# Every eighth row product of a PEER gather moved from VectorE to GpSimd and ScalarE

## The chip, the cores and the metric

The kernel runs on one core of a Trainium2 chip. The metric is device time in microseconds (us) for one execution, the median of several runs.

## The reference, cut to what matters

One decoder layer is computed for 1024 prompt tokens and 8 sample tokens: a retention and a sliding-window attention group, an output projection, and then the PEER block, whose inner part is what the change touches. For each token, eight heads pick 16 of 16384 experts each, so 128 experts per token, and

```python
h = jnp.einsum('thkd,td->thk', peer_u[idx], xt)
a = jax.nn.gelu(h, approximate=False) * gates
return jnp.einsum('thk,thkd->td', a, peer_v[idx])
```

with d = 1024 in float32. Each token thus needs 128 rows of `peer_u` and 128 rows of `peer_v`. The kernel has the two tables side by side, one row of 8 KB per expert.

## The kernel before, in words

The prompt's tokens are worked in 8 blocks (`NB`) of 128, one token per partition. In each block there are 128 *units* (`SLOTS`): a unit is one expert for each of the 128 tokens. Its row pair (u beside v, 128 partitions x 8 KB, 1 MB in all) is fetched by one indirect DMA that GpSimd issues (`fetch`, line 657) into one of 8 places of a ring (`RING`; place r = unit % 8). Tokens are split between even and odd units so that each fetch brings rows for two half sets; hence the two operand tiles `xlo` and `xhi`, for even and odd units.

A unit then goes through four engines:

- VectorE, `expert_dot` (line 1943): waits for the row's landing (`ld_row[r]`), multiplies the u half by the token (`xlo` or `xhi`) and adds up along the row in the same instruction, into `dot[:, r]`. After each odd unit it raises `dots`, one count per pair of units.
- ScalarE, `weigh` (line 1402), once per pair p: waits for `dots`, takes the gelu of both sums, and writes two 128x64 diagonals over the u half of the row. It raises `diags`.
- TensorE, `add_pair` (line 1093, matmuls at line 1097), once per pair: waits for `diags` and adds diagonal times v half into the block's sum in PSUM, eight matmuls by the profile's count. Each of the two units raises `used` with its last matmul.
- GpSimd: for unit u it waits for `used` to say that unit u - 8 is done with the place, and issues the next fetch.

GpSimd's program (line 676 on) is one plain loop over blocks, quarters and units. At the start of each quarter of 32 units it also waits for the picked indices to be moved (`moved`) and copies them (`take_picks`, line 669, with a wait for its own copy). It does nothing else until the 8 fetches for the sample tokens at the end.

All other work of the layer (projections of later tiles, the attention of the next block, the picking of its experts, the output norm) is interleaved by hand in ticks: after each unit or pair an engine calls `advance`, which runs the steps that fall due at that tick. So TensorE's program order is pair, other work, pair, other work, and the same holds on VectorE and ScalarE; nothing is reordered at run time. Plain loads and stores are issued from the SP queue, by the same ticks.

At the start of a block, `take_over` on VectorE (line 1930) and `take_halves` on ScalarE (line 1417) wait for all dots of the block before, since they overwrite `xlo` and `xhi`.

Of the kernel before, what the change touches and what calls it, by code (L numbers as in the profile page):

```python
# [9 lines left out]
ALU = mybir.AluOpType  # L10
# [3 lines left out]
P = 128  # L14
# [127 lines left out]
def build(nc, A, out):  # L142
    ctx = ExitStack()
    with ctx:
# [3 lines left out]
        def sem(name):  # L148
            return ctx.enter_context(nc.semaphore(name))
# [174 lines left out]
        ld_first, ld_const, ld_skT = sem("ld_first"), sem("ld_const"), sem("ld_skT")  # L324
        ld_g1, ld_xT_first, ld_xT_early = sem("ld_g1"), sem("ld_xT_first"), sem("ld_xT_early")
        ld_wq = [sem(f"ld_wq{i}") for i in range(QG)]
# [31 lines left out]
        halves_taken = sem("halves_taken")  # L358
        head_moved = sem('head_moved')
        moved = [sem(f"moved{i}") for i in range(QTR)]  # L360
        ld_row = [sem(f"ld_row{r}") for r in range(RING)]
# [25 lines left out]
        def _(sp):  # L387
# [161 lines left out]
            sp.dma_start(xT_first, A["xT"][0]).then_inc(ld_xT_first, 16)  # L549
            sp.dma_start(g1c, A["norm1_g"].rearrange("(k p) -> p k", p=P), allow_slow_non_contiguous=True).then_inc(ld_g1, 16)  # L550
            load_w(0)
# [102 lines left out]
        def _(pool):  # L654
# [6 lines left out]
            picks_in = stage[:].bitcast(U32)  # L661

            def take_first_head():

                hold(pool, head_moved, 32)
                nc.gpsimd.tensor_copy(idxg[:, 0, :, 0:HPAIRS], picks_in[:, 0, :, 0, 0:HPAIRS]).then_inc(idx_taken, 1)
                hold(pool, idx_taken, 1)
# [10 lines left out]
            for b in range(NB):  # L678
                for quarter in range(QTR):
                    if b == quarter == 0:  # L680
                        take_first_head()
                    else:
                        take_picks(b, quarter, 0)
                    for unit in range(quarter * QSLOTS, (quarter + 1) * QSLOTS):
                        if b == 0 and unit == 2 * HPAIRS:
                            take_picks(0, 0, HPAIRS)
                        if b == 0 and unit == RING // 2:
                            hold(pool, pj_mm, NCH + AHEAD)
                        hold(pool, used, b * SLOTS + (unit + 1))
                        pick = unit // 2 % QPAIRS  # L690
                        fetch(unit % RING, idxg[:, quarter, unit % 2, pick:pick + 1])

            pool.wait_ge(sm["idx8"], 1)
# [460 lines left out]
        def _(act):  # L1154
# [247 lines left out]
            def weigh(b, p):  # L1402
                r = 2 * p % RING
                act.wait_ge(dots, b * PAIRS + (p + 1))
                me.did(nc.scalar.activation(gel[:, r:r + 2], dot[:, r:r + 2], ACT.Gelu))  # L1405
                me.sync()
# [10 lines left out]
            def take_halves(b):  # L1417

                if b:
                    act.wait_ge(dots, b * PAIRS)  # L1420
                    act.nop(nofuse=True)
                act.wait_ge(x2_swapped, b + 1)
# [66 lines left out]
        def _(v):  # L1489
# [78 lines left out]

            v.wait_ge(ld_g1, 16)
            v.nop(nofuse=True)  # L1570
            v.wait_ge(ld_xT_first, 16)
            gain(xT_first)
# [357 lines left out]
            def take_over(b):  # L1930

                if b:
                    v.wait_ge(dots, b * PAIRS)
                    v.nop(nofuse=True)
                v.wait_ge(x2_swapped, b + 1)
                me.did(nc.vector.tensor_copy(xlo[0:HP, :], x2[0:HP, :]))
# [6 lines left out]
            def expert_dot(b, unit):  # L1943
# [3 lines left out]
                          accum_out=dot[:, r:r + 1])  # L1947
                if unit % 2:
                    ins.then_inc(dots, 1)
# [31 lines left out]
            for b in range(NB):  # L1981
                take_over(b)
                for unit in range(SLOTS):
                    expert_dot(b, unit)
                    if b and unit == 3:
# [156 lines left out]
```

## Time and profile before

| what | value |
|---|---|
| median of 3 runs | 2977.24 us (2976.3 to 2979.08) |
| the profiled execution's own time | 2974.54 us |
| its span | 2972.7 us |
| PE, DVE, ACT, POOL busy | 2245.8, 2075.9, 1094.1, 1207.3 us |
| DMA | 1214.41 MB, mean 409 GB/s |
| mean granted TensorE clock | 0.871 of full speed |

PE is TensorE (PEld its weight loads), DVE VectorE, ACT ScalarE, POOL GpSimd, SP the queue of plain DMAs. A time is that of one profiled execution, counted from its span's start. "Idle before" a row, and what follows the arrow, is the time the engine stood still before that instruction and what ended it. The 1024 units of the ring run from about 131 us to 2946 us, which is 2815 us, 2.75 us a unit; before it lies the first tile's front, behind it the sample tokens' end.

### The profile page before, as it was taken

Reading aid. Unit: us, or ns where it says so; the run is one execution under the profiler, and the core shown is the slowest. Engines: PE = TensorE matmul, PEld = TensorE weight load, DVE = VectorE, ACT = ScalarE, POOL = GpSimd, SP = SyncE. Lnnn points to the kernel's source line nnn. Section 1 sums busy time; section 2 is a strip of 40 time slices with the busy share of each in tenths; the row PEclk is TensorE's granted clock in tenths of the full one; section 3 lists DMA queues with packets and bytes.
Section 4 is the critical chain, followed back from the end, with each engine's and each line's share of the span. In section 5 each row is a group of like instructions: output and inputs, shape, how many; then the busy total and the mean of one; then the engine's idle time right before and its main releaser. Section 6 shows DMA issues by size and latency. Waiting matters only on the chain.

```text
span 2972.7 us, 33489 instructions
## 1 busy us (share of the span) xinstructions
PE 2245.8 (76%) x10572; PEld 1116.2 (38%) x10572; DVE 2075.9 (70%) x5291; ACT 1094.1 (37%) x3330; POOL 1207.3 (41%) x1069
## 2 busy tenths in 40 slices
PE   8898888566899678996776676866786568778755
PEld 6666534122466224662343232512242123314211
DVE  3685458964786557865578865797569865986975
ACT  2233433352343433433434352343434353332322
POOL 0133344444433343334444444444444444544453
PEclk9999889889999788997898788977898789977776
DMA  9999999999999999999999999999999999999998
GB/s 366 381 418 408 399 421 420 408 421 420 416 397 396 424 420 414 400 386 410 421 421 396 421 405 419 421 409 421 415 421 418 411 412 417 420 405 381 412 415 353
DMA packets 197043, 1214.41 MB, mean 409 GB/s; under 512 B 28320, under 2 KB 47592, under 8 KB 63104
## 3 DMA queue, kind: packets, MB, share of 16 engines
q0 software_dynamic: 148608, 1082.20, 88.4%
q1 hardware_dynamic: 48256, 130.07, 11.2%
q8 instruction: 83, 1.36, 0.2%
q14 instruction: 96, 0.79, 0.1%
HBM read 1192.48 MB, written 20.23 MB: 408 GB/s over the span
## 4 chain that ended last, share of the span: by engine, by line
DMA 36%; DVE 28%; PE 23%; issue 5%; ACT 5%; POOL 2%; DVEq 0%; SPq 0%; POOLq 0%; ACTq 0%
DMA ring<-in_peer_uv,idxg 29%; DVE ring L1946 15%; PE ps L1097 11%; PE ps L751 5%; DVE columns L1779 3%; DMA proj_scratch<-wo 3%; POOL ring L657 2%; DVE columns L1773 2%; PE ps L1050 2%; ACT ring L1158 2%; DMA wo<-in_xT_sample 1%; DVE columns L1785 1%; PE ps L1000 1%; DVE columns L1849 1%; PE ps L724 1%
## 5 line engine op out<-in xcount | busy, mean ns | idle before, releaser
L657 POOL DMA_INDIRECT ring<-in_peer_uv,idxg x1024 | 1185.4, 1158 | 1613.1 <-PE ps L1097 1417.3
L1097 PE MATMUL ps<-ring 128*64 128x512 f32 x4096 | 1227.3, 729 | 659.3 <-ACT ring L1158 647.2
L1946 DVE SCALAR_TENSOR_TENSOR ring<-ring,xlo 128x1024 f32<-128x1024 f32 x512 | 627.5, 1226 | 367.6 <-DMA ring<-in_peer_uv,idxg 323.2
L1946 DVE SCALAR_TENSOR_TENSOR ring<-ring,xhi 128x1024 f32<-128x1024 f32 x512 | 627.4, 1225 | 322.7 <-DMA ring<-in_peer_uv,idxg 300.6
L1097 PEld LDWEIGHTS ps<-ring 128*64 128x64 f32 x4096 | 285.1, 156 | 1357.8 <-ACT ring L1158 928.1
L1405 ACT ACTIVATE small<-small 128x2 f32<-128x2 f32 x512 | 103.8, 203 | 1494.2 <-DVE ring L1946 1479.8
L1050 PEld LDWEIGHTS ps<-work,wq 128*128 128x128 f32 x2304 | 274.0, 196 | 87.8 <-issue 86.5
L1158 ACT ACTIVATE ring<-gdiag,small 128x64 f32<-128x64 f32 x1024 | 300.3, 340 | 16.8
L1158 ACT ACTIVATE gdiag<-fold,gateg 128x64 f32<-128x64 f32 x1024 | 293.0, 333 | 3.0
L1050 PE MATMUL ps<-work,wq 128*128 128x128 f32 (+1 forms) x2304 | 292.9, 281 | 1.1 <-ACT work L1158 1.1
L751 PE MATMUL ps<-wo 128*128 128x176 f32 x1680 | 272.9, 320 | 13.7 <-ACT wo L1158 6.0
L751 PEld LDWEIGHTS ps<-wo 128*128 128x128 f32 x1680 | 255.1, 193 | 60.1 <-issue 45.3
L1773 DVE MAX8 columns<-columns 128x8 f32<-128x128 f32 (+3 forms) x432 | 116.8, 324 | 41.7 <-ACT columns L1158 37.4
L1779 DVE FIND_INDEX8 columns<-columns 128x8 uint32<-128x128 f32 (+3 forms) x432 | 135.3, 328 | 0.0
L1000 PE MATMUL ps<-wo,work 128*128 128x512 f32 x224 | 109.4, 621 | 0.0
L1405 ACT ACT_TABLE_LOAD x82 | 105.2, 1283 | 1.5
L1158 ACT ACTIVATE wo<-ps,small 128x176 f32<-128x176 f32 (+1 forms) x96 | 40.1, 422 | 148.9 <-PE ps L751 94.7
L1158 ACT ACTIVATE columns<-ps 128x512 f32<-128x512 f32 (+2 forms) x98 | 54.0, 560 | 60.0 <-PE ps L1050 40.4
L1000 PEld LDWEIGHTS ps<-wo,work 128*128 128x128 f32 x224 | 40.0, 193 | 72.4 <-issue 72.4
L1785 DVE MATCH_REPLACE8 columns<-columns 128x128 f32<-128x128 f32 (+3 forms) x216 | 66.9, 319 | 0.0
L1849 DVE TENSOR_TENSOR columns<-columns 128x256 f32<-128x256 f32 (+1 forms) x144 | 54.9, 420 | 2.6
L1852 DVE TENSOR_REDUCE columns<-columns 128x32 f32<-128x512 f32 (+2 forms) x74 | 49.6, 670 | 2.5
(214 smaller groups left out, 1580.9 us busy)
## 6 DMA issues: line engine op xcount, KB each, us to landing
wo<-in_w_in SPq DMA_DIRECT2D x41, 704.0 KB
ring<-in_peer_uv,idxg POOLq DMA_INDIRECT x1024
wo<-in_w_out SPq DMA_DIRECT2D x4, 4096.0 KB, 17.1
ring<-in_w_in SPq DMA_DIRECT2D x8, 1408.0 KB, 7.4
wq<-in_w_q SPq DMA_DIRECT2D x4, 2048.0 KB, 25.2
proj_scratch<-wo SPq DMA_DIRECT2D x93, 88.0 KB
columns<-proj_scratch SPq DMA_DIRECT2D x7, 896.0 KB
h<-in_x_prompt SPq DMA_DIRECT2D x9, 512.0 KB, 7.9
```

What stands on the lines that cost most here:

```text
L657: nc.gpsimd.indirect_dma_start(row[r], None, A["peer_uv"], bass.IndirectOffsetOnAxis(ap=experts, axis=0)).then_inc(ld_row[r], 16)
L751: mm = nc.tensor.matmul(o, tokens_T(n, k), w[:, k, :], start=(k == 0), stop=(k == KC - 1))
L1000: mm = nc.tensor.matmul(F[2 + n][0:rows, :], lhsT, weights[:, k, n * 512:(n + 1) * 512], start=(k == 0), stop=(k == KC - 1))
L1050: mm = nc.tensor.matmul(bank_of(b, n, c)[:, c * P:c * P + rows], wq[:, n, k, c * P:(c + 1) * P], xT[:, k * P:k * P + rows], start=(k == 0) ...
L1097: mm = nc.tensor.matmul(acc[side * HP:(side + 1) * HP, n * 512:(n + 1) * 512], row_u[r][:, 0:HP], row_v[r][:, n * 512:(n + 1) * 512], star ...
L1158: return nc.scalar.activation(o, i, ACT.Copy, **kw_)
L1405: me.did(nc.scalar.activation(gel[:, r:r + 2], dot[:, r:r + 2], ACT.Gelu))
L1773: me.did(nc.vector.max(v16(j)[:, r8 * 8:r8 * 8 + 8], rowsof(j)))
L1779: me.did(nc.vector.max_index(i16(j)[:, r8 * 8:r8 * 8 + 8], v16(j)[:, r8 * 8:r8 * 8 + 8], rowsof(j)))
L1785: me.did(nc.vector.match_replace(rowsof(j), v16(j)[:, 0:8], rowsof(j), TAKEN))
L1849: me.did(tt(o3, o3, i4[:, h0 + hh, c, :].rearrange("p (a k) -> p a k", a=1) .to_broadcast([rows, TK, TK]), ALU.mult))
L1946: ins = stt(row_u[r], row_u[r], 1.0, (xlo, xhi)[unit % 2][:], ALU.mult, ALU.mult, accum_out=dot[:, r:r + 1])
```

## The change

Of every eight units the last (place 7) is taken from VectorE. GpSimd multiplies its u half by `xhi`, in place, and ScalarE adds the products up with a copy that has an accumulator, before its gelu. GpSimd does this between its fetches: after the fetch of the unit with place 5 of the next round, six units later, and for a block's last unit right after that unit's own fetch. `take_over` and `take_halves` also wait for the block's GpSimd products. Apart from this, the first load of the norm weights now raises the same semaphore as the load beside it, which frees one semaphore.

```diff
-            sp.dma_start(g1c, ...).then_inc(ld_g1, 16)
+            sp.dma_start(g1c, ...).then_inc(ld_xT_first, 16)
...
+            def expert_dot(b, unit):
+
+                r = unit % RING
+                hold(pool, halves_taken, b + 1)
+                hold(pool, x2_taken, b + 1)
+                hold(pool, ld_row[r], b * (ROUNDS * 16) + (unit // RING * 16 + 16))
+                nc.gpsimd.tensor_tensor(row_u[r], row_u[r], xhi[:], ALU.mult).then_inc(pool_dots, 1)
...
                         fetch(unit % RING, idxg[:, quarter, unit % 2, pick:pick + 1])
+                        if unit >= RING and unit % RING == RING - 3:
+                            expert_dot(b, unit + 2 - RING)
+                expert_dot(b, SLOTS - 1)
...
             def weigh(b, p):
                 r = 2 * p % RING
                 act.wait_ge(dots, b * PAIRS + (p + 1))
+                if p % (RING // 2) == RING // 2 - 1:
+                    act.nop(nofuse=True)
+                    act.wait_ge(pool_dots, b * ROUNDS + (p // (RING // 2) + 1))
+                    me.did(nc.scalar.activation(row_u[r + 1], row_u[r + 1], ACT.Copy, accum_out=dot[:, r + 1:r + 2]))
+                    me.sync()
...
                 if b:
                     act.wait_ge(dots, b * PAIRS)
+                    act.nop(nofuse=True)
+                    act.wait_ge(pool_dots, b * ROUNDS)
...
-            v.wait_ge(ld_g1, 16)
-            v.nop(nofuse=True)
-            v.wait_ge(ld_xT_first, 16)
+            v.wait_ge(ld_xT_first, 32)
...
                     v.wait_ge(dots, b * PAIRS)
                     v.nop(nofuse=True)
+                    v.wait_ge(pool_dots, b * ROUNDS)
+                    v.nop(nofuse=True)
...
-                if unit % 2:
+                if unit % 2 or unit % RING == RING - 2:
                     ins.then_inc(dots, 1)
...
-                    expert_dot(b, unit)
+                    if unit % RING < RING - 1:
+                        expert_dot(b, unit)
```

## Rows read from the trace of the kernel before

**Rows 1.** The page's DMA line over 40 slices, and its busiest queue.

```profile
DMA  9999999999999999999999999999999999999998
...
q0 software_dynamic: 148608, 1082.20, 88.4%
```

**Rows 2.** The page's chain that ended last, by line.

```profile
DMA ring<-in_peer_uv,idxg 29%; DVE ring L1946 15%; PE ps L1097 11%; PE ps L751 5%; DVE columns L1779 3%; DMA proj_scratch<-wo 3%; POOL ring L657 2%; DVE columns L1773 2%; PE ps L1050 2%; ACT ring L1158 2%; DMA wo<-in_xT_sample 1%; DVE columns L1785 1%; PE ps L1000 1%; DVE columns L1849 1%; PE ps L724 1%
```

**Rows 3.** The page's costliest groups: count, busy us, mean ns, idle before.

```profile
L657 POOL DMA_INDIRECT ring<-in_peer_uv,idxg x1024 | 1185.4, 1158 | 1613.1 <-PE ps L1097 1417.3
L1097 PE MATMUL ps<-ring 128*64 128x512 f32 x4096 | 1227.3, 729 | 659.3 <-ACT ring L1158 647.2
L1946 DVE SCALAR_TENSOR_TENSOR ring<-ring,xlo 128x1024 f32<-128x1024 f32 x512 | 627.5, 1226 | 367.6 <-DMA ring<-in_peer_uv,idxg 323.2
```

**Rows 4.** Windows: length, busy (count) per engine, granted clock, DMA share, GB/s.

```profile
131.00:2946.00 2815.00, 2125.61 (x9953) 1029.97 (x9953) 1996.80 (x5079) 1054.07 (x3246) 1197.80 (x1056) 0.87 1.01 412
345.07:396.12 51.05, 31.85 (x105) 10.72 (x104) 19.96 (x34) 12.33 (x44) 18.38 (x17) 0.77 1.01 424
396.12:436.27 40.15, 31.00 (x121) 12.28 (x120) 23.29 (x39) 14.16 (x45) 20.89 (x19) 0.87 1.01 421
436.27:478.23 41.96, 36.23 (x226) 22.93 (x225) 32.48 (x93) 11.87 (x43) 18.19 (x16) 0.96 1.01 421
478.23:521.31 43.08, 34.99 (x172) 17.01 (x172) 39.51 (x120) 21.37 (x56) 20.26 (x17) 0.90 1.01 419
```

**Rows 5.** The same four windows, instructions of line 1097 alone (PE, PEld).

```profile
345.07:396.12 51.05, 20.61 (x64) 4.73 (x64) 0.77 1.01 424
396.12:436.27 40.15, 18.16 (x64) 4.27 (x64) 0.87 1.01 421
436.27:478.23 41.96, 16.64 (x65) 3.98 (x65) 0.96 1.01 421
478.23:521.31 43.08, 18.70 (x64) 4.44 (x64) 0.90 1.01 419
```

**Rows 6.** Timeline, places 4 to 7 of a round: start, duration, instruction.

```profile
426.81 2.00 PE L1097 MATMUL ps<-ring 128*64 128x512 f32 x8
...
428.50 1.23 DVE L1946 SCALAR_TENSOR_TENSOR ring<-ring,xhi 128x1024 f32<-128x1024 f32 x1 [1.21 <-DMA ring<-in_peer_uv,idxg]
...
429.76 0.20 ACT L1405 ACTIVATE small<-small 128x2 f32<-128x2 f32 x1 [1.82 <-DVE ring L1946]
...
430.64 1.94 PE L1097 MATMUL ps<-ring 128*64 128x512 f32 x8 [1.83 <-ACT ring L1158]
...
430.83 0.94 POOL L657 DMA_INDIRECT ring<-in_peer_uv,idxg  x1 [0.30 <-issue]
```

**Rows 7.** GpSimd's copies of indices: ns min/median/max by line.

```profile
L672 POOL COPY idxg<-stage x32: 203/219/1210, 156.4 to 2850.9; 128x32 uint32<-128x32 uint32 x31, 128x16 uint32<-128x16 uint32 x1
L666 POOL COPY idxg<-stage x1: 196/196/196, 118.7 to 118.7; 128x16 uint32<-128x16 uint32 x1
```

**Rows 8.** Timeline, one such copy and VectorE's instruction beside it.

```profile
1413.63 0.86 POOL L672 COPY idxg<-stage 128x32 uint32<-128x32 uint32 x1
...
1413.22 1.22 DVE L1946 SCALAR_TENSOR_TENSOR ring<-ring,xlo 128x1024 f32<-128x1024 f32 x1
```

**Rows 9.** ScalarE's copy of 1024 columns and its read of an accumulator, by form.

```profile
L1158 ACT ACTIVATE work<-ps 128x1024 f32<-128x1024 f32 x32 | 32.2, 1008 | 9.1 <-PE ps L702 5.6 <-PE ps L1097 3.5
...
L1251 ACT ACTIVATION_READ_ACCUMULATOR h<-h,small 128x1 f32 x32 | 6.0, 187 | 0.0
```

**Rows 10.** Timeline: GpSimd's first copy and fetch; a fetch into an empty queue.

```profile
118.73 0.20 POOL L666 COPY idxg<-stage 128x16 uint32<-128x16 uint32 x1 [118.28 <-DMA stage<-moving]
119.89 1.10 POOL L657 DMA_INDIRECT ring<-in_peer_uv,idxg  x1 [0.97 <-POOL idxg L666]
...
1330.32 1.03 POOL L657 DMA_INDIRECT ring<-in_peer_uv,idxg  x1 [8.07 <-PE ps L1097]
...
1335.87 1.23 DVE L1946 SCALAR_TENSOR_TENSOR ring<-ring,xlo 128x1024 f32<-128x1024 f32 x1 [5.32 <-DMA ring<-in_peer_uv,idxg]
```

More of the change, by code:

```diff
@@ L324, in build @@
         ld_first, ld_const, ld_skT = sem("ld_first"), sem("ld_const"), sem("ld_skT")
-        ld_g1, ld_xT_first, ld_xT_early = sem("ld_g1"), sem("ld_xT_first"), sem("ld_xT_early")
+        ld_xT_first, ld_xT_early = sem("ld_xT_first"), sem("ld_xT_early")
         ld_wq = [sem(f"ld_wq{i}") for i in range(QG)]
@@ L359, in build @@
         head_moved = sem('head_moved')
+        pool_dots = sem('pool_dots')
         moved = [sem(f"moved{i}") for i in range(QTR)]
@@ L549, in _ @@
             sp.dma_start(xT_first, A["xT"][0]).then_inc(ld_xT_first, 16)
-            sp.dma_start(g1c, A["norm1_g"].rearrange("(k p) -> p k", p=P), allow_slow_non_contiguous=True).then_inc(ld_g1, 16)
+            sp.dma_start(g1c, A["norm1_g"].rearrange("(k p) -> p k", p=P), allow_slow_non_contiguous=True).then_inc(ld_xT_first, 16)
             load_w(0)
```

## The prediction

> **What bounds the kernel now.** I read the page's DMA line first. It is at nine tenths or more in all but the last slice, and GpSimd's queue of fetches alone takes 88.4% of the 16 engines' span [rows 1]. The windows say it more sharply: over the 2815 us in which the ring runs, the DMA share is 1.01 [rows 4]. So the DMA engines bound the kernel, and the busy shares of VectorE and TensorE are of work that has to fit beside the rows. The chain that ended last goes through VectorE's dot for 15% [rows 2], which would speak for relieving VectorE, but over the same stretch the DMA engines hardly rest, so most of that chain runs beside transfers that set the pace anyway. Then I read the groups for who waits: GpSimd waits 1417.3 us in total for TensorE to free a place, TensorE 647.2 us for ScalarE's diagonals [rows 3]. This is a loop: fetch, land, dot, gelu and diagonal, matmuls, fetch. The ring's eight places cover its latency now. The question is how much the change adds to the loop and how much is in reserve.
>
> **The round, as the change makes it.** Call the four pairs of a round of eight places A, B, C, D; D holds places 6 and 7. In the row of before, C's matmuls end at 428.81; the fetch that goes to place 5 starts at 430.83 and ends at 431.77, while D's matmuls have begun at 430.64 [rows 6]. D starts 1.13 us before that fetch ends. With the change, D cannot start before that fetch has ended, GpSimd has multiplied, and ScalarE has added up. From C's end to D's start there is now a fixed path B:
> - C's end to the end of the fetch to place 5: 431.77 - 428.81 = 2.96 us [rows 6]; with the wait behind it some 3.0.
> - The product on GpSimd. No row shows a GpSimd tensor_tensor of 128x1024. Bounds: VectorE does it in 1.23 us [rows 3], the lower end. GpSimd copies 16 columns in 196 ns and 32 in 203 to 219 ns [rows 7], so 0.4 to 1.4 ns a column; 1024 columns of two operands would be 0.9 to 2.9 us, with the fixed 0.2 us up to 3.1 us, the upper end. I take 2.4 us, two passes at VectorE's 1.2 ns a column, since VectorE's row has the same shape. The copy beside VectorE's two-operand instruction says why two passes: it took 0.86 us and ended at 1414.49, just as VectorE's ended at 1414.44, where such a copy alone takes 0.2 us [rows 7, 8]. GpSimd's reads wait for VectorE's, so they share a way in. For that wait I add 0.3 us: VectorE's dot fills about half of the time of a unit (1.23 of 2.75 us), and half a dot is 0.6 us.
> - ScalarE's sum: 1.01 us for 1024 columns and 0.19 us for the accumulator, 1.2 us [rows 9].
> - From gelu to D's first matmul: 430.64 - 429.76 = 0.9 us [rows 6]; three hand-overs of 0.1 us between engines (428.50 + 1.23 = 429.73 to 429.76 and the like).
> B = 3.0 + 0.3 + 2.4 + 1.2 + 0.9 + 0.3 = 8.1 us.
>
> The Trainium skill, "GPSIMD Engine Reference", Performance versus the Vector engine, gives 4497 ns for a tensor_tensor of 2048 columns, by my halving an estimate of 2.25 us; nothing in this trace shows it, and with it the sum below would be some 16 us lower (0.9 us in half a block, 1.2 us at the ends).
>
> **What a round then takes.** TensorE's program is fixed: A, other work, B, other work, C, other work, D, other work. Only the other work between C and D can lie inside the 8.1 us. With W TensorE's busy time in a stretch, O what of it is not line 1097, a quarter of O lies there, so a stretch of n rounds needs W - O/4 + 8.1 n. I take half a block, 345 to 521 us, whose 176.2 us is the mean length of a sixteenth of 2815; each window has two rounds (64 matmuls of line 1097) [rows 4, 5]:
> - 51.05 us: 31.85 - 11.24/4 + 16.2 = 45.2, so 5.8 to spare;
> - 40.15 us: 31.00 - 12.84/4 + 16.2 = 44.0, 3.8 too long;
> - 41.96 us: 36.23 - 19.59/4 + 16.2 = 47.5, 5.6 too long;
> - 43.08 us: 34.99 - 16.29/4 + 16.2 = 47.1, 4.0 too long.
> The ring holds one round, so what a window has to spare is not saved for the next: 13.4 us are lost in half a block, 16 x 13.4 = 215 us. If it could be saved, the whole ring would say 2125.6 - 898.3/4 + 128 x 8.1 = 2937.8 against 2815 us, 123 us lost [rows 3, 4]; that is the low side of this term.
>
> **The ends of blocks.** GpSimd's product of unit 127 stands right behind that unit's own fetch, and waits for its landing. Queued behind it are the next block's index copy and all its fetches; today they go out while the last rows still land. So the queue runs empty, 7 times between blocks and once before the sample rows. From the time unit 127 could be multiplied: 0.1 hand-over, 2.4 product, 0.2 copy, 0.96 from the copy's end to the fetch, and from a fetch into an empty queue to its dot 1335.87 - 1330.32 = 5.55 us [rows 10]; 9.2 us, where rows now follow each other at 2.75. Lost: 6.45 us each, 52 us. Those 8 rounds are counted in the term above too, at 1.7 us each: 13 back.
>
> **The rest.** VectorE loses 128 dots, 157 us busy; nothing waits for it that the DMA engines would not make wait, since their share is already 1.01: I give it nothing. In the densest window VectorE is at 39.5 of 43.1 us; even if it stands still for both of GpSimd's products there, it has 39.5 + 2 x (2.4 - 1.23) = 41.8 us, below the 47.1 above. ScalarE gains 154 us on 1054 and stays the least used. The added waits in the takeovers lie in the emptied queue's 9.2 us. The merged semaphore waits for the same two loads: nothing; its cover is that both were waited for already. The added cost of a lower clock (0.77 where TensorE was busy 62% of a window, 0.96 at 86%, rows 4) as TensorE idles more is left to the range.
>
> **Sum.** 215 + 52 - 13 = 254 us on the profiled execution's 2974.5, which stands 2.7 under the median: 3231, rounded to 3230 us.
>
> **Rivals.**
> 1. *Only the ends of blocks cost.* The ring's depth hides the late D. The condition is a B under which the windows above have room: the third breaks first, at (41.96 - 31.33)/2 = 5.3 us. For it: GpSimd's product could be at its low end and its fetch to place 5 shorter, as VectorE no longer holds it there. Against: 3.0 + 1.2 + 0.9 + 0.3 are 5.4 before any product. Time: 2977 + 52 - 7 = 3022.
> 2. *The port.* GpSimd's product waits for VectorE's instructions not now and then but nearly each time a whole one, 1.2 us more: B = 9.3. Then the windows give -3.4, 6.2, 8.0, 6.4: 20.6 x 16 = 330, and 8 x 7.6 = 61 for the ends, less 21: 3347. For it: the copy of rows 8, and VectorE busy 32 of 42 and 40 of 43 us in two windows. Against: in the other two it is busy half the time. The Trainium skill, "SBUF — State Buffer", Who interferes with whom, has that a VectorE instruction with two SBUF inputs and a GpSimd one that reads SBUF exclude each other for the whole instruction; by that rule, this is the case, and the trace's 0.86 us copy agrees.
> 3. *VectorE's relief wins (the other side).* Where the chain goes through line 1946, 15% of the span, one eighth of it leaves: 56 us, 2921 us. It decides where VectorE ends last and the DMA engines have room; it needs a DMA share well under 1 there and a B under 5.3. The share of 1.01 in all four windows speaks against it.
> 4. *The change does little*: GpSimd's products hide and the ends overlap other traffic. 2977. Against: the order in GpSimd's program leaves no way around the last unit's landing.
>
> **Chances.** Forecast 0.70 (3230), rival 1 0.09, rival 2 0.16, rival 3 0.03, rival 4 0.02. The product at its lower end, 1.2 us, gives B = 6.9 and 6.2 x 16 = 100, ends 42, less 6: 3113; at its upper end, 3.1, B = 8.8 and 282 + 57 - 18: 3298. The range takes in both and most of rival 2: 3100 to 3350. A measurement of this kernel tells about 0.2% from no change: faster 0.03, same 0.02, slower 0.95.
>
> **What would show it.** Right: 128 GpSimd multiplies of about 2.4 us; DMA share in the ring near 0.92 with engines all but idle for some 6 us at seven block ends; TensorE's wait for line 1158 and ScalarE's for GpSimd grown; D 8 us behind C. Wrong: multiplies of 1.2 us, or D soon behind C with the DMA share still 1.01 inside blocks (rival 1), or VectorE's two-operand dots stretched beyond 1.23 us and setting the pace (rival 2).

## The result: slower by 429 us

| | before | after |
|---|---|---|
| median of the runs, us | 2976.77 (4 runs, 2970.0 to 2979.08) | 3406.08 (4 runs, 3401.77 to 3410.06) |
| ratio, 95% interval | | 1.1438 [1.1416, 1.146] |
| profiled execution's own time, its span | 2974.5, 2972.7 | 3405.99, 3404.2 |
| mean granted TensorE clock | 0.871 | 0.815 |

The direction and the path that costs the time came out as forecast, the size did not: 254 us were forecast, 429 measured, which is 175 us more and outside the range.

The page of the changed kernel answers to [rows 1] with a DMA line that is under nine tenths in 16 of its 40 slices, and a queue of fetches that fell from 88.4% to 80.4% for the same packets and bytes:

```profile
PEclk9989888778898778987886778867887788877776
DMA  9999998999898998899998999798888998898897
...
q0 software_dynamic: 148608, 1082.20, 80.4%
```

The chain that ended last, by engine, has GpSimd at 14%, and TensorE's line 1109 (1097 of before) at 24% where [rows 2] had it at 11%:

```profile
PE 43%; DMA 14%; POOL 14%; ACT 10%; DVE 10%; issue 9%; SPq 1%; POOLq 0%; DVEq 0%; ACTq 0%
PE ps L1109 24%; DMA ring<-in_peer_uv,idxg 12%; POOL ring L670 7%; POOL ring L658 6%; PE ps L763 6%; DVE ring L1965 5%; PE ps L1062 5%; ACT ring L1420 3%; PE ps L1012 3%; ACT ring L1170 3%; DMA wo<-in_xT_sample 1%; ACT L1422 1%; ACT small L1422 1%; DMA ring<-in_w_in 1%; PE ps L1070 1%
```

The page's groups, beside [rows 3]: TensorE's idle time before its pair matmuls rose from 659.3 to 1025.2 us, and their busy time from 1227.3 to 1277.5. The two new groups are GpSimd's product (line 670) and ScalarE's sum (line 1420), which waits for it 1015.3 us in total:

```profile
L1109 PE MATMUL ps<-ring 128*64 128x512 f32 x4096 | 1277.5, 761 | 1025.2 <-ACT ring L1170 1025.0
L658 POOL DMA_INDIRECT ring<-in_peer_uv,idxg x1024 | 1137.3, 1111 | 1711.9 <-PE ps L1109 1483.3
L1965 DVE SCALAR_TENSOR_TENSOR ring<-ring,xlo 128x1024 f32<-128x1024 f32 x512 | 700.6, 1369 | 613.1 <-DMA ring<-in_peer_uv,idxg 572.6
...
L1965 DVE SCALAR_TENSOR_TENSOR ring<-ring,xhi 128x1024 f32<-128x1024 f32 x384 | 514.9, 1341 | 190.3 <-DMA ring<-in_peer_uv,idxg 176.8
L1420 ACT ACTIVATE ring<-ring 128x1024 f32<-128x1024 f32 x128 | 135.2, 1057 | 1026.3 <-POOL ring L670 1015.3
L670 POOL TENSOR_TENSOR ring<-ring,xhi 128x1024 f32<-128x1024 f32 x128 | 305.2, 2384 | 81.0 <-DMA ring<-in_peer_uv,idxg 78.7
```

The window of the whole ring, to set beside the first of [rows 4], says the rest: DMA share 0.91 for 1.01, granted clock 0.81 for 0.87, and TensorE busy 2189 of 3240 us.

```profile
131.00:3371.00 3240.00, 2188.85 (x9947) 1063.37 (x9945) 2024.92 (x4821) 1192.99 (x3497) 1452.59 (x1180) 0.81 0.91 357
```

The timeline of one round, from the matmuls of pair C to those of pair D, answers to [rows 6] and shows the forecast path term by term:

```profile
482.75 1.94 PE L1109 MATMUL ps<-ring 128*64 128x512 f32 x8
...
485.46 0.94 POOL L658 DMA_INDIRECT ring<-in_peer_uv,idxg  x1 [1.65 <-PE ps L1109]
...
486.70 0.93 POOL L658 DMA_INDIRECT ring<-in_peer_uv,idxg  x1 [0.30 <-issue]
487.66 2.35 POOL L670 TENSOR_TENSOR ring<-ring,xhi 128x1024 f32<-128x1024 f32 x1
490.04 1.06 ACT L1420 ACTIVATE ring<-ring 128x1024 f32<-128x1024 f32 x1 [9.24 <-POOL ring L670]
491.00 0.19 ACT L1420 ACTIVATION_READ_ACCUMULATOR ring<-ring 128x1 f32 x1
491.22 0.20 ACT L1422 ACTIVATE small<-small 128x2 f32<-128x2 f32 x1
...
492.09 3.68 PE L1109 MATMUL ps<-ring 128*64 128x512 f32 x8 [4.53 <-ACT ring L1170]
492.42 0.57 ACT L1170 ACTIVATE columns<-ps 128x512 f32<-128x512 f32 x1
...
493.10 0.88 DVE L1790 MAX8 columns<-columns 128x8 f32<-128x128 f32 x4 [13.73 <-ACT columns L1170]
```

C ends at 484.69, the second fetch at 487.63 (2.94 us, forecast 2.96), the product takes 2.35 (forecast 2.4), the sum is over at 491.19 (1.15 after the hand-over, forecast 1.2), and D starts 0.87 after gelu (forecast 0.9). Two things in these rows are not in the forecast. D's eight matmuls take 3.68 us where C's took 1.94. And ScalarE, standing 9.24 us before the sum, holds what is queued behind it: its copy of `columns` comes at 492.42 only, and VectorE stood 13.73 us for it.

The windows of C, of the stretch between, and of D give the granted clock in their last but two column: 1.00 (2.4 GHz), then 0.81 with TensorE busy 1.56 of 6 us, then 0.50 (1.2 GHz).

```profile
482.75:484.69 1.94, 1.94 (x10) 0.56 (x9) 0.00 (x0) 0.00 (x0) 0.94 (x1) 1.00 1.00 418
486.00:492.00 6.00, 1.56 (x14) 1.37 (x13) 0.00 (x0) 1.90 (x6) 3.68 (x3) 0.81 1.00 381
492.09:495.77 3.68, 3.68 (x9) 0.84 (x9) 2.57 (x11) 0.91 (x3) 0.00 (x0) 0.50 0.77 323
```

**A round, averaged.** One row is one round; the trace has 127 whole ones. I took from each the duration of the four pairs' matmuls and the gaps between them, and of each gap what TensorE filled with other work; the rest is waiting. In us:

| mean over the rounds | A | gap | B | gap | C | gap C to D | D | gap | round |
|---|---|---|---|---|---|---|---|---|---|
| before | 2.32 | 3.17 | 2.40 | 3.08 | 2.47 | 2.99 | 2.41 | 3.17 | 22.0 |
| after | 2.17 | 2.29 | 2.16 | 2.52 | 2.23 | 8.13 | 3.50 | 2.36 | 25.4 |
| after, waiting in the gap | | 0.61 | | 0.86 | | 6.34 | | 0.32 | 8.1 |

The path from C's end to D's start is 8.13 us on the mean, forecast 8.1. That mean is made of two kinds of round: 8.36 us in 120 of the 128, and 4.75 in the last round of each block, where the product stands behind its own unit's fetch and not behind C. The round is 3.35 us longer; times 127 this is 425 of the 429 us. The waiting in the four gaps of a round also adds up to 8.13 us, which is chance; times 127 it is 1032 us, close to the group's 1025.2.

### The profile page after: what moved, and what is told of

The parts are those of the page before. It is cut to its first block, busy times and chain, and to the rows that moved or that the text cites. A ratio compares the mean times of both kernels' runs of the same rounds, so it can differ in the third digit from the quotient of the medians.

```text
span 3404.2 us, 34133 instructions
## 1 busy us (share of the span) xinstructions
PE 2314.2 (68%) x10572; PEld 1151.0 (34%) x10572; DVE 2104.0 (62%) x5035; ACT 1234.2 (36%) x3586; POOL 1466.4 (43%) x1197
## 3 DMA queue, kind: packets, MB, share of 16 engines
q0 software_dynamic: 148608, 1082.20, 80.4%
## 4 chain that ended last, share of the span: by engine, by line
PE 43%; DMA 14%; POOL 14%; ACT 10%; DVE 10%; issue 9%; SPq 1%; POOLq 0%; DVEq 0%; ACTq 0%
PE ps L1109 24%; DMA ring<-in_peer_uv,idxg 12%; POOL ring L670 7%; POOL ring L658 6%; PE ps L763 6%; DVE ring L1965 5%; PE ps L1062 5%; ACT ring L1420 3%; PE ps L1012 3%; ACT ring L1170 3%; DMA wo<-in_xT_sample 1%; ACT L1422 1%; ACT small L1422 1%; DMA ring<-in_w_in 1%; PE ps L1070 1%
## 5 line engine op out<-in xcount | busy, mean ns | idle before, releaser
L1109 PE MATMUL ps<-ring 128*64 128x512 f32 x4096 | 1277.5, 761 | 1025.2 <-ACT ring L1170 1025.0
L658 POOL DMA_INDIRECT ring<-in_peer_uv,idxg x1024 | 1137.3, 1111 | 1711.9 <-PE ps L1109 1483.3
L1965 DVE SCALAR_TENSOR_TENSOR ring<-ring,xlo 128x1024 f32<-128x1024 f32 x512 | 700.6, 1369 | 613.1 <-DMA ring<-in_peer_uv,idxg 572.6
L1109 PEld LDWEIGHTS ps<-ring 128*64 128x64 f32 x4096 | 305.3, 165 | 1724.8 <-ACT ring L1170 1228.3
L1965 DVE SCALAR_TENSOR_TENSOR ring<-ring,xhi 128x1024 f32<-128x1024 f32 x384 | 514.9, 1341 | 190.3 <-DMA ring<-in_peer_uv,idxg 176.8
L1420 ACT ACTIVATE ring<-ring 128x1024 f32<-128x1024 f32 x128 | 135.2, 1057 | 1026.3 <-POOL ring L670 1015.3
L670 POOL TENSOR_TENSOR ring<-ring,xhi 128x1024 f32<-128x1024 f32 x128 | 305.2, 2384 | 81.0 <-DMA ring<-in_peer_uv,idxg 78.7
L1866 DVE TENSOR_TENSOR columns<-columns 128x256 f32<-128x256 f32 (+1 forms) x144 | 74.7, 558 | 2.6
```

The source lines that it names most:

```text
L658: nc.gpsimd.indirect_dma_start(row[r], None, A["peer_uv"], bass.IndirectOffsetOnAxis(ap=experts, axis=0)).then_inc(ld_row[r], 16)
L670: nc.gpsimd.tensor_tensor(row_u[r], row_u[r], xhi[:], ALU.mult).then_inc(pool_dots, 1)
L1109: mm = nc.tensor.matmul(acc[side * HP:(side + 1) * HP, n * 512:(n + 1) * 512], row_u[r][:, 0:HP], row_v[r][:, n * 512:(n + 1) * 512], star ...
L1420: me.did(nc.scalar.activation(row_u[r + 1], row_u[r + 1], ACT.Copy, accum_out=dot[:, r + 1:r + 2]))
L1965: ins = stt(row_u[r], row_u[r], 1.0, (xlo, xhi)[unit % 2][:], ALU.mult, ALU.mult, accum_out=dot[:, r:r + 1])
```

## The experiments

Each is the changed kernel with the edit shown. Times are medians of four executions (seven in run 9, twelve in run 10); the kernel before ran in each set too, with medians of 2974.2 to 2980.1 us, and the ratios are against it. A difference between two times is good to some 10 us or more, as the intervals show.

**1. The block's last product moved.** The product of unit 127 is made after the next block's fetch to place 5, so nothing is queued behind its landing.

```diff
-                        if unit >= RING and unit % RING == RING - 3:
-                            expert_dot(b, unit + 2 - RING)
-                expert_dot(b, SLOTS - 1)
+                        if unit % RING == RING - 3:
+                            if unit >= RING:
+                                expert_dot(b, unit + 2 - RING)
+                            elif b:
+                                expert_dot(b - 1, SLOTS - 1)
```

> The changed kernel, but a block's last product (unit 127) is made after the next block's fetch to place 5, as in every other round, and the last block's after the sixth sample fetch. Theory A (the time is lost in the wait inside each round; the block ends cost what was forecast): the seven gaps between a block's last fetch and the next block's first, 11.8 us now against 4.7 us in the kernel before, close by some 7 us each, 45 to 55 us less than the 3406 of the changed kernel, so about 3355. Rival (the missing 176 us are at the block ends, where ScalarE and VectorE also wait for the last product): 150 us less or more, below 3260.

Measured 3394.5 us, ratio 1.1395 [1.1357, 1.1432]: 12 us back by the medians, and its interval still touches that of the changed kernel. Both the 45 to 55 us of theory A and the 150 of the rival are missed. The queue does run empty at a block's end. This is one in the changed kernel, from its timeline and windows; GpSimd waits 6.89 us for the landing, the next fetch goes out at 558.37, and the DMA share is about a half for 17 us:

```profile
546.36 1.31 POOL L658 DMA_INDIRECT ring<-in_peer_uv,idxg  x1 [0.30 <-issue]
554.56 2.36 POOL L670 TENSOR_TENSOR ring<-ring,xhi 128x1024 f32<-128x1024 f32 x1 [6.89 <-DMA ring<-in_peer_uv,idxg]
556.86 0.67 POOL L681 COPY idxg<-stage 128x32 uint32<-128x32 uint32 x1
558.37 1.01 POOL L658 DMA_INDIRECT ring<-in_peer_uv,idxg  x1 [0.83 <-POOL idxg L681]
```

```profile
546.00:557.00 11.00, 10.43 (x58) 4.95 (x57) 10.55 (x25) 1.81 (x7) 3.81 (x4) 1.00 0.54 191
557.00:563.00 6.00, 1.94 (x8) 0.48 (x8) 3.28 (x6) 5.87 (x11) 4.25 (x5) 1.00 0.49 168
```

But in a kernel that no longer moves rows at the DMA engines' pace, an empty queue costs little: TensorE is busy 10.43 of the 11 us in which it drains and 1.94 of the 6 behind, together 12.37 of 17, more than its mean of 2189 in 3240. The block ends are not where the missing time is.

**2 to 4. The path made shorter.** ScalarE's sum over 64 columns, GpSimd's product over 64, and both.

```diff
-                    me.did(nc.scalar.activation(row_u[r + 1], row_u[r + 1], ACT.Copy, accum_out=dot[:, r + 1:r + 2]))
+                    me.did(nc.scalar.activation(row_u[r + 1][:, 0:64], row_u[r + 1][:, 0:64], ACT.Copy, accum_out=dot[:, r + 1:r + 2]))
```

```diff
-                nc.gpsimd.tensor_tensor(row_u[r], row_u[r], xhi[:], ALU.mult).then_inc(pool_dots, 1)
+                nc.gpsimd.tensor_tensor(row_u[r][:, 0:64], row_u[r][:, 0:64], xhi[:, 0:64], ALU.mult).then_inc(pool_dots, 1)
```

> ScalarE adds up only 64 of the 1024 products; 960 are left out of the sum. GpSimd's product is whole. This takes about 0.7 us (1.06 to some 0.34) out of the path from C's end to D's start and touches no port that VectorE or GpSimd use. Theory A (each us of that path costs a us per round, 128 rounds): 85 to 95 us less, about 3315. Theory P (a good part of the time is VectorE standing still while GpSimd multiplies): the same or less than that, as the product is untouched. Rival (the ring hides part of the path): under 50 us less.

> GpSimd multiplies only 64 of the 1024 columns; the other 960 are left as they landed. ScalarE's sum is whole. About 2.1 us less on the path (2.35 to some 0.25) and 2.1 us less in which GpSimd can shut VectorE out. Theory A: the same gain per us as the shorter sum, 128 x 2.1 = 270 us less, about 3140. Theory P: more per us than the shorter sum gains, as VectorE's instructions, 185 us longer in all than 7/8 of those of before, go back to 1.23 us: 330 to 400 us less, 3010 to 3080.

> Product and sum both over 64 columns only, the other 960 left out of both. The order of the programs and all waits stay. Path from C to D 8.1 - 2.1 - 0.7 = 5.3 us, which the forecast gave as the point where the loop has room again. Theory A: what is left over the kernel before is the block ends with a product of 0.25 us, 7 x 5 us, so 3000 to 3030. Rival (waiting in this order costs by itself, since ScalarE's and VectorE's other work is queued behind the wait): 3060 or more.

| run | gap C to D, us | D's matmuls, us | time, us | ratio |
|---|---|---|---|---|
| changed kernel | 8.13 | 3.50 | 3406.1 | 1.1438 [1.1416, 1.146] |
| sum over 64 | 7.35 | 3.40 | 3332.3 | 1.1193 [1.1157, 1.1229] |
| product over 64 | 6.17 | 3.23 | 3205.2 | 1.0776 [1.0733, 1.0819] |
| both | 5.40 | 3.08 | 3142.7 | 1.0558 [1.0523, 1.0593] |

The sum's edit gives 74 us for 0.78 us of path, the product's 201 for 1.96, both 263 for 2.73: 95, 103 and 96 us for each us. Within the noise (some 13 us on the 74 and on the 201) a microsecond of ScalarE's is worth as much as one of GpSimd's, so it is the length of the path that costs, far more than GpSimd's hold on VectorE. The gains stay under what the expectations had (85 to 95 and 270 us), in part because the product over 64 columns takes 0.55 and 0.52 us on the mean and not 0.25. And at 5.40 us, next to the 5.3 at which the forecast had the loop find room again, 163 us over the kernel before are still left: theory A (3000 to 3030) fails here, and the rival's 3060 or more came true.

A microsecond a round would be 128 us, and 95 to 103 came back. By the averages over rounds the rest turns up as waiting elsewhere: TensorE's waits before A, B and C together are 1.8 us a round in the changed kernel, 2.1 with the shorter sum, 2.4 with the shorter product, 2.6 with both, and 4.1 in the kernel before.

**5 and 6. The product moved to place 3.** GpSimd makes the product after the fetch to place 3 (behind pair B) instead of 5; in 6 the block's last product is moved as in 1 as well. Both compute all that the reference does.

```diff
-                        if unit >= RING and unit % RING == RING - 3:
-                            expert_dot(b, unit + 2 - RING)
+                        if unit >= RING and unit % RING == RING - 5:
+                            expert_dot(b, unit + 4 - RING)
```

> The changed kernel with the product of place 7 made two fetches earlier: after the fetch to place 3 of the next round (after pair B's matmuls) and not after that to place 5 (after C's). Four runs so far give 93 to 103 us per us between C's end and D's start (3406 us at 8.13, 3332 at 7.35, 3205 at 6.17, 3143 at 5.40). Theory A (that path sets the time): 8.1 us now count from B's end, and other work, C and other work, 1.8 + 2.2 + 1.8 us, lie inside; D starts some 4 us after C's end; on the line of the four runs this is about 3010 to 3040. Rival (GpSimd now waits for the landing of row 7 with two fetches queued behind, and starves the DMA engines every round): no better than 3300.

> The same, and a block's last product after the next block's fetch to place 3. With the product late, moving the block's end was worth only 12 us, where the forecast had 52. Theory: a gap in the fetches costs in full only where the DMA engines set the pace; with the product early they do so again, so here it is worth more, 30 to 50 us less than with the early product alone, 2975 to 3005, about the kernel before. Rival: the ends are cheap in any case: 15 us less or under.

Measured 3058.15 us, ratio 1.0286 [1.0251, 1.032], and 3023.84, ratio 1.0161 [1.0132, 1.0189], each some 20 us above its expected range. The mean gap C to D falls to 4.63 and 4.73 us. GpSimd's product now runs beside TensorE's work; this is the timeline of the first, in which C starts at 495.45, 1.33 us before the product, and D at 501.24:

```profile
495.45 1.94 PE L1109 MATMUL ps<-ring 128*64 128x512 f32 x8
495.55 1.21 POOL L658 DMA_INDIRECT ring<-in_peer_uv,idxg  x1 [0.30 <-issue]
496.78 2.37 POOL L670 TENSOR_TENSOR ring<-ring,xhi 128x1024 f32<-128x1024 f32 x1
499.18 1.06 ACT L1420 ACTIVATE ring<-ring 128x1024 f32<-128x1024 f32 x1 [4.00 <-POOL ring L670]
...
501.24 1.94 PE L1109 MATMUL ps<-ring 128*64 128x512 f32 x8 [0.97 <-ACT ring L1170]
```

So 348 of the 429 us hang on the place of the product in GpSimd's program. The block ends, worth 12 us in the changed kernel, are worth 34 here, where the DMA engines set the pace again (share 1.00 in the ring of 6, below). Run 6 is the best full form of the change that was tried, and it is still slower than the kernel before by 1.6%, 50 us. These were not taken apart further.

```profile
131.00:2990.00 2859.00, 2127.91 (x9929) 1041.32 (x9929) 1956.28 (x4814) 1196.36 (x3486) 1534.83 (x1177) 0.86 1.00 404
```

**7. Shorter dots on VectorE**, those of places 2 to 5 over 64 columns, and **12. all seven over 64 columns.** What is left out is the product of the other columns.

```diff
-                ins = stt(row_u[r], row_u[r], 1.0, (xlo, xhi)[unit % 2][:], ALU.mult, ALU.mult,
+                n = 64 if 2 <= r < 6 else D
+                ins = stt(row_u[r][:, 0:n], row_u[r][:, 0:n], 1.0, (xlo, xhi)[unit % 2][:, 0:n], ALU.mult, ALU.mult,
```

> The changed kernel with VectorE's dots of places 2 to 5 over 64 of the 1024 columns, the other 960 left out of these four sums. GpSimd's and ScalarE's part is whole. In the changed kernel TensorE still waits 230 us in all before pairs A, B and C, where the forecast had none. Theory V (VectorE, with its dots and the front's steps in one order, is what is late there, and it cannot make use of the time in which D is waited for): most of it goes, 130 to 200 us less, 3210 to 3280. Rival L (the rows land late, or ScalarE is late): under 60 us less.

> The changed kernel with all seven of VectorE's dots over 64 of the 1024 columns, 960 left out of each sum; GpSimd's product and ScalarE's sum are whole. Shorter dots at places 2 to 5 were worth 92 us, and TensorE's waits before A, B and C went from 1.8 to 1.4 us a round. Theory V (these waits come from VectorE): 40 to 80 us less again than that run's 3314, 3235 to 3275, with B after A and C after B at 2.0 us or less. Rival L (what is left are rows that land late): 3300 or more.

Measured 3313.64 us, ratio 1.1136 [1.1108, 1.1165], which is 92 us less than the changed kernel and between what the two theories gave; and 3276.36, ratio 1.1017 [1.0979, 1.1054], 130 us less, just outside theory V's 3235 to 3275. The groups of run 12, all of VectorE's dots at 0.35 to 0.37 us:

```profile
L1109 PE MATMUL ps<-ring 128*64 128x512 f32 x4096 | 1250.5, 747 | 933.7 <-ACT ring L1170 916.4
L658 POOL DMA_INDIRECT ring<-in_peer_uv,idxg x1024 | 979.6, 957 | 1748.4 <-PE ps L1109 1517.5
L1966 DVE SCALAR_TENSOR_TENSOR ring<-ring,xlo 128x64 f32<-128x64 f32 x512 | 189.9, 371 | 1013.9 <-DMA ring<-in_peer_uv,idxg 974.2
```

The 130 us are of three kinds. The waiting before A, B and C falls from 1.79 to 1.39 us a round, 51 us. The gap C to D falls from 8.13 to 7.75, 48 us; most of it fits the two fetches in the path, which take 957 ns on the mean beside short dots and 1111 beside long ones. The rest is TensorE's matmuls, 27 us. So VectorE's dots are one cause, but only part of the gain is waiting outside the path: with the dots all but gone 1.39 us a round are left, and of these 177 us in that trace I could put 101 down to rows that had not landed when VectorE asked for them (64 in the changed kernel).

**8 to 10. Nobody waits for the product.** The diff shows ScalarE's part. The sum of place 7 is left out and ScalarE waits for the row's landing instead; GpSimd's product, over columns 64 to 1023, only has to end before the next fetch into its place. In 9 the block's last product is also moved as in 1; 10 is 9 with a product of 64 columns, so that hardly more than VectorE's relief is left.

```diff
-                    act.wait_ge(pool_dots, b * ROUNDS + (p // (RING // 2) + 1))
-                    me.did(nc.scalar.activation(row_u[r + 1], row_u[r + 1], ACT.Copy, accum_out=dot[:, r + 1:r + 2]))
-                    me.sync()
+                    act.wait_ge(ld_row[r + 1], b * (ROUNDS * 16) + (2 * p // RING * 16 + 16))
+                    act.nop(nofuse=True)
```

> The product stays in GpSimd's program, over columns 64 to 1023, but nothing in the round waits for it: ScalarE neither waits for it nor adds it up (it waits for the row's landing), so the sum of place 7 is left out; only the next fetch into the place and the block's end wait for the product. VectorE has seven dots of eight. What remains over the kernel before is GpSimd's time, its shutting VectorE out, and the block ends. Theory A: the block ends alone, 30 to 50 us over the kernel before, 3010 to 3030. Theory P (VectorE is shut out at GpSimd's multiplies and this sets the pace): 3080 or more. If VectorE's relief were worth anything, it shows here: below 2977.

> As the run in which nothing in the round waits for the product (3042 us), with a block's last product made after the next block's fetch to place 5; the sum of place 7 is left out again, and GpSimd multiplies columns 64 to 1023. This takes the block ends away and leaves GpSimd's multiplies and what they shut out. Theory: block ends are worth 30 to 50 us here, since the DMA engines set the pace: 2995 to 3010, and what is then left over 2974 is the port. Rival: no port cost, 2974 to 2985.

> The same with GpSimd's multiply over 64 columns, so that it takes some 0.25 us and shuts nobody out: what is left is VectorE with seven dots of eight, and nothing in their place. The forecast gave VectorE's relief nothing, since the DMA share was 1.01: within 8 us of the kernel before. Rival (the chain that ended last, with 15% in VectorE's dot, was to be believed): 56 us less, about 2920. If the multiplies' port cost is real, this is below the run beside it by that cost.

| run | time, us | ratio |
|---|---|---|
| 8, no wait | 3042.11 | 1.0222 [1.0195, 1.0249] |
| 9, and block ends moved | 3011.06 | 1.0096 [1.0061, 1.0131] |
| 10, relief alone | 2975.2 | 0.9988 [0.9974, 1.0002] |

Without the wait 364 of the 429 us are gone, though GpSimd still multiplies 960 of the 1024 columns; the 3042 lie between what theories A and P gave. From 9 to 10 the product shrinks from 960 to 64 columns and 36 us go: this is about what GpSimd's time and its hold on VectorE cost where the DMA engines set the pace (run 9's executions spread from 2988.59 to 3022.5 us). Run 10 comes near the most that the change could gain, with only a product of 483 ns in place of the dot, and its interval takes in 1. The page and the ring's window of run 10 show why: VectorE is busy 1853 us where it was 1997 [rows 4], and the DMA share is 1.01 as it was:

```profile
DMA  9999999999999999999999999999999999999998
```

```profile
131.00:2935.00 2804.00, 2113.10 (x9945) 1028.34 (x9941) 1853.04 (x4821) 1053.43 (x3241) 1227.01 (x1182) 0.87 1.01 413
```

**11, 13 and 14. D's clock.** Matmuls of a block of zeros, which add exact zeros, ahead of each D: 10, 6 and 3 of them, each two instructions in the trace. TensorE's program also waits at its start for the loads of the two operands, which the diff leaves out.

```diff
+                if p % (RING // 2) == RING // 2 - 1:
+                    for i in range(FILL):
+                        nc.tensor.matmul(acc[0:HP, i % 2 * 512:(i % 2 + 1) * 512], dmaskT[HP:P, 0, 0:HP], g2b[HP:P, 0:512],
+                                         start=False, stop=False, skip_group_check=True)
```

> The changed kernel, with ten matmuls by a block of zeros in TensorE's program ahead of each pair D (two calls' worth of rows each, about 0.5 us a call at full clock, 5 us in all), in the time in which TensorE waits for the product. They add zero to the block's sum. Theory C (TensorE's idling lets the clock fall, so that D's matmuls take 3.5 us and not 2.2, and this is a part of the missing time): D's matmuls come down to 2.0 to 2.5 us, and the time by 100 to 150 us, to 3260 to 3310. Rival (the slower D is hidden, as other waits take its place): under 40 us less, or more than 3406, as the zeros come in the way of pairs that are not late.

> The changed kernel with 6 zero-block matmuls (of 512 columns, adding exact zeros) ahead of each D on TensorE, instead of the 10 of the run before. They do not change what is computed. In the run with 10 they took 8.8 us, longer than the wait that they were to fill; 6 of them should take some 5.3 us, which ends inside the wait of 6.3 us of the changed kernel, and the places ahead of them in TensorE's order are as before. Theory (D at the lower clock is a part of the missing time: its matmuls take 3.5 us instead of 2.2 because TensorE has idled): D's matmuls run at the higher clock, near 2.0 to 2.4 us, and the run is some 100 us faster than the changed kernel, near 3300 us; a longer other work behind C costs part of it. Rival (the clock follows the waits and costs nothing, since other waits take up what D gains): 3400 or more. A third outcome: the fills are themselves slow at the lower clock, still push D, and the run is slower than 3406, which would leave the size of the term open again.

> The same with 3 zero-block matmuls ahead of each D, some 2.6 us, which leaves TensorE idle for 3 to 4 us before D. Theory (the clock that D gets depends on how long TensorE has idled before it): D's matmuls at or near the lower clock, 3.0 to 3.5 us, and the run within 1% of the changed kernel, 3380 to 3430 us. If 3 are enough to keep D at 2.4 us, the run is as fast as with 6 or faster, 3280 to 3330 us. Rival (clock costs nothing): 3400 to 3430 whatever D's duration.

| matmuls of zeros | gap C to D, us | D's matmuls, us | C's end to D's end, us | time, us | ratio |
|---|---|---|---|---|---|
| none | 8.13 | 3.50 | 11.63 | 3406.1 | 1.1438 [1.1416, 1.146] |
| 3 | 8.19 | 3.31 | 11.50 | 3388.7 | 1.1376 [1.1347, 1.1406] |
| 6 | 9.04 | 2.71 | 11.75 | 3413.0 | 1.1468 [1.1434, 1.1502] |
| 10 | 11.77 | 2.17 | 13.94 | 3617.9 | 1.2089 [1.2007, 1.217] |

With 10 the filling outlasts the wait (11.49 us of the gap are work), and the run misses its theory: 212 us slower instead of some 100 faster (its executions spread from 3581.01 to 3640.24 us). With 3, the time and D's duration are as the theory had them (3380 to 3430, 3.0 to 3.5), but the rival's 3400 is only 11 us off. With 6 the total is what the rival or the third outcome gave; but the timeline and windows of that run show D at a granted clock of 1.00 behind TensorE's unbroken work, where the changed kernel has 0.50 behind a stretch of little of it:

```profile
486.77 5.36 PE L1108 MATMUL ps<-g2b,dmaskT 64*64 64x512 f32 x12
486.94 2.35 POOL L671 TENSOR_TENSOR ring<-ring,xhi 128x1024 f32<-128x1024 f32 x1
...
492.06 1.94 PE L1114 MATMUL ps<-ring 128*64 128x512 f32 x8
```

```profile
486.77:492.06 5.29, 5.29 (x13) 1.52 (x12) 0.00 (x0) 2.68 (x8) 2.49 (x2) 1.00 1.01 401
492.06:494.00 1.94, 1.94 (x10) 0.55 (x9) 1.52 (x5) 0.21 (x1) 0.00 (x0) 1.00 0.83 351
```

The filling held D back by 0.91 us a round and the clock gave 0.79 back. Were D's duration free, the 0.91 us would have cost 87 us by the 96 us for each us of runs 2 to 4; 7 were measured. So D's duration counts much like the wait ahead of it, though not it alone: the other work behind D is 0.2 us a round shorter too. For runs that change the path or fill it, the column that orders them is C's end to D's end. Against it, the changed kernel's distance to the others is: sum over 64, 74 us for 0.88; product over 64, 201 for 2.23; both, 263 for 3.15; place 3 (4.63 + 2.90), 348 for 4.10; 10 matmuls, 212 for 2.31. That is 84 to 92 us for each us in five runs. Runs 1, 7 and 12, which change something else, are not on this line: 12, 92 and 130 us less at 11.90, 11.61 and 11.27 us. By 87, the line drawn on comes down to the kernel before at 11.63 - 429 / 87 = 6.7 us; the kernel before has 2.99 + 2.41 = 5.40, so by this estimate its reserve was 1.3 us a round. No full run lies between 7.5 and 5.4 us.

## Why the prediction was right in kind and wrong in size

**Right: what bounds the kernel before, and the relief.** VectorE's relief was put at nothing; run 10 gives 0.9988 [0.9974, 1.0002].

**Right: the path of 8.1 us.** The mean gap is 8.13, and 8.36 in the 120 rounds in which the whole path lies behind C: 3.64 us from C's end to the product (forecast 3.3 with the wait at the port), 2.39 for it (2.4), 2.33 from there to D (2.4). That the mean over all rounds is nearer still is luck, as the last round of each block has 4.75. The product's minimum, median and maximum, with the row of VectorE's odd dots, are:

```profile
L1965 DVE SCALAR_TENSOR_TENSOR ring<-ring,xhi x384: 1174/1225/3909, 128.4 to 3359.7; 128x1024 f32<-128x1024 f32 x192
...
L670 POOL TENSOR_TENSOR ring<-ring,xhi x128: 2340/2351/2756, 149.9 to 3366.1; 128x1024 f32<-128x1024 f32 x128
```

The 2.4 us taken from two passes at VectorE's rate measured 2.35. The 4497 ns for 2048 columns of the Trainium skill, "GPSIMD Engine Reference", Performance versus the Vector engine, halved, gave an estimate of 2.25. The 0.3 us for the wait at the port did not fall on the product, whose mean is 0.03 over its median, but in part on the fetches ahead of it (1111 ns on the mean, 0.93 to 0.94 us undisturbed).

**Wrong: the step "What a round then takes".** It counted a stretch of n rounds as W - O/4 + 8.1 n: all of TensorE's work back to back, with no wait but the one before D, and every matmul as long as before. Two of its assumptions failed.
- *No wait outside the path.* In the kernel before, TensorE waits 1.3 to 1.4 us before each of the four pairs. The step let the three outside the path go to nothing; 0.61, 0.86 and 0.32 are left, 1.79 us a round, 227 us in all. Going back from each late pair to the gelu and the dot before it, I could put about 141 of these us down to VectorE being busy, 64 to rows that had not landed and 22 to ScalarE; run 12 confirms the first only in part (51 us back, with landings taking over). ScalarE's program stands behind its wait for the product, the front's copies in it included, and VectorE's front work stands with it: the wait of line 1790 for ScalarE's copy, 13.73 us in the round shown. How much of the 141 us that queueing makes was not tried.
- *D as long as before.* It takes 3.50 us for 2.41, at the lower of the two clock levels in the round shown; in 101 of the 128 rounds it takes over 3.5 us, where the kernel before has 19 such. A, B and C together are 0.63 shorter. Net this is 0.46 x 127 = 58 us; by the 87 us for each us that the runs give, D's own 1.09 us is worth about 95. The forecast saw the clock fall and left it to the range, and that was too little.

The sum as measured: the step's own figure for the whole ring, 123 us; the waits, 227; the pairs' matmuls, 58; other work outside the path, which takes 5.38 us a round where the step had 5.26, 15; the path's 0.03 us, 4. These are 427 us for the 425 by which the 127 rounds are longer. The block ends, 12 us by run 1, are no further term, since their waits are in the 227. The forecast took 215 for the first of these, by windows of half a block in which room was not saved for the next; by this account that figure was 92 too high, and it hid a part of what the step left out.

**The point at which the path decides** was put at a B of 5.3 us, by the same step. With both parts of the path cut to 5.40 us, 163 us remained, and the line reaches the kernel before at 6.7 us from C's end to D's end, which at D's usual 2.4 is a B of 4.3, or 3.7 by the gap alone (429 / 96 = 4.5 us below 8.13). Both are drawn on from longer paths.

**The ends of blocks, 52 us**, were over-sized here: 12 us in the changed kernel, 31 to 34 where the DMA engines set the pace (runs 8 to 9 and 5 to 6). The term was made against DMA engines that are the bound, in a kernel whose round the same forecast made longer than their work.

**The rivals.** Rival 1 (only the block ends) falls with run 1. Rival 2 (the port) has its mechanism in the trace, but not its size: 36 us between runs 9 and 10, and the path's cost per us is, within the noise, no higher for the product than for ScalarE's sum. Its 3347 us lay nearer to the result for a reason that did not hold: it lengthened the path to 9.3 us, and the path was 8.13. Rival 3 (relief wins) falls with run 10, and rival 4 with the result.

## What to carry to other kernels

A helper engine's work that lies in a ring's loop lengthens the loop by its whole in-order path, here fetch, product, sum and diagonal; each us of it cost about 0.7 us a round (84 to 92 us in 128 rounds) once the loop set the pace. The place in the helper's program decides: the same product one pair earlier gave 348 of 429 us back. Before counting on a ring's depth, compare the loop's waits now (here 1.3 us before each pair) with the path added; do not assume that the waits elsewhere go to nothing, nor that TensorE's work keeps its duration after a long pause. And work taken from VectorE, busy 1997 of 2815 us, was worth nothing here, since the DMA engines set the pace.

## What the runs showed of the hardware

- **GpSimd's product holds some of VectorE's instructions up until it ends, and others not at all.** In the changed kernel's timeline an instruction on 32 columns takes 2.47 us while its like, right behind, takes 0.17. In another round a dot of 1.22 us takes 3.15: the product ends at 342.76, and the dot about its own length later, at 343.85. Over the whole trace, of the instructions that overlap a product, all 13 TENSOR_TENSOR of 128x256, all 4 CAST of 64x16 and 6 of 7 TENSOR_SCALAR of 128x32 are stretched, but none of 36 MAX8, MATCH_REPLACE8, FIND_INDEX8 and TENSOR_REDUCE. The product itself keeps near its 2.35 us (median; 2.76 at most).

```profile
512.51 2.47 DVE L1845 TENSOR_SCALAR columns<-columns 128x32 uint32<-128x32 uint32 x1
512.58 2.35 POOL L670 TENSOR_TENSOR ring<-ring,xhi 128x1024 f32<-128x1024 f32 x1
514.89 0.17 DVE L1846 TENSOR_SCALAR columns<-columns 128x32 uint32<-128x32 uint32 x1
...
340.39 2.37 POOL L670 TENSOR_TENSOR ring<-ring,xhi 128x1024 f32<-128x1024 f32 x1
340.70 3.15 DVE L1965 SCALAR_TENSOR_TENSOR ring<-ring,xhi 128x1024 f32<-128x1024 f32 x1
```

  The Trainium skill, "SBUF — State Buffer", Who interferes with whom, has that `tensor_scalar` can take the shared ports and that the second one to issue waits for the whole instruction. The blocking agrees. The order can't be read here: in 35 cases the one held up starts first in the trace, by up to 0.57 us, but in some of them it would by its usual length have been over before the product's recorded start (0.42 us for an instruction 0.57 us ahead), so the recorded starts don't tell when the blocking began. GpSimd's fetch is recorded as ending 0.02 us before the product in these cases.
- **D ran at half the clock after the pause in the round shown**, 3.68 us for 1.94, with a granted clock of 0.50 for 1.00, and 3.50 us on the mean of all rounds; six matmuls of zeros in the pause kept it at 1.00 in the round shown (mean 2.71 us). D took under 2.1 us in 7 of 128 rounds without zeros, in 18 with three (mean 3.31 us), in 65 with six and in 107 with ten.
- **A short product on GpSimd is not short in proportion**: 128x64 took 522 ns on the mean in run 4, against 2384 for 128x1024. From 483 ns for 64 columns in run 10 and 2262 for 960 in run 9, an estimate is 1.99 ns a column and 0.36 us fixed.
- **A fetch takes GpSimd longer beside VectorE's dots.** In the kernel before, the 742 fetches that overlap a dot by more than 0.1 us take 1.23 us on the mean and the 290 others 0.97. With all dots over 64 columns (run 12) the mean of the ring's 1024 is 957 ns.
